# Gate and up weights of an expert in two runs of a slot in place of interleaved columns

## The reference

```python
def hier_moe(h, w_grp, b_grp, w_rtr, b_rtr, w_gate, w_up, w_down):
    ...                                   # gates: (tokens, 16), two of them not zero
    a = jnp.einsum('td,edf->tef', t, w_gate)      # w_gate, w_up: (16, 1024, 256) for a layer
    u = jnp.einsum('td,edf->tef', t, w_up)
    hid = jax.nn.silu(a) * u * gates.astype(t.dtype)[..., None]
    y = jnp.einsum('tef,efd->td', hid, w_down)    # w_down: (16, 256, 1024)
```

## Time and profile before

| | |
|---|---|
| median of 3 runs | 1561.44 us (1558.87 to 1562.86) |
| profiled execution: time, span | 1561.03 us, 1559.2 us |
| mean granted TensorE clock | 0.914 of full speed |
| busy: DVE, ACT, POOL | 46%, 26%, 15% of the span |
| q1 (SP's loads): packets, bytes | 111264, 175.39 MB |
| q0 (POOL's DMAs): packets, bytes | 21344, 70.08 MB |

### The profile page before, as it was taken

The page is one execution under the profiler, slowest core; times in us unless marked ns, Lnnn a source line. Parts: engine busy times, 40 slices in busy tenths (PEclk is TensorE's granted clock), DMA queues, the critical chain, the costliest instruction groups (busy, mean ns, idle before and its releaser), DMA issues.

```text
span 1559.2 us, 23096 instructions
## 1 busy us (share of the span) xinstructions
PE 1292.1 (83%) x8094; PEld 773.3 (50%) x8094; DVE 709.6 (46%) x1687; ACT 410.1 (26%) x929; POOL 229.4 (15%) x358
## 2 busy tenths in 40 slices
PE   4899978999998589888478998799999945986950
PEld 3455455777676444333244454577766733532420
DVE  0345425777544524232346443377664444422326
ACT  2110145666401111010121112466761100100112
POOL 3310111000111012210211100200002001110023
PEclk8899989999999689999879999899999966998985
DMA  9500577000314844999470014910004073299943
GB/s 334 205 13 1 184 267 199 1 2 28 122 41 156 312 157 118 359 378 381 174 271 12 1 37 157 321 29 1 20 10 149 28 270 107 83 362 381 367 165 146
DMA packets 132760, 247.54 MB, mean 159 GB/s; under 512 B 6688, under 2 KB 80672, under 8 KB 128512
## 3 DMA queue, kind: packets, MB, share of 16 engines
q1 hardware_dynamic: 111264, 175.39, 33.0%
q0 software_dynamic: 21344, 70.08, 12.6%
HBM read 217.17 MB, written 28.38 MB: 157 GB/s over the span
## 4 chain that ended last, share of the span: by engine, by line
PE 43%; DVE 9%; DMA 5%; issue 4%; SPq 3%; DVEq 1%; ACT 1%; POOL 0%; POOLq 0%; ACTq 0%
PE ps L2049 8%; PE ps L1767 8%; PE ps L1663 5%; PE ps L1946 4%; PE ps L2094 4%; PE ps L1826 3%; PE ps L2043 3%; PE ps L1879 3%; DMA ring<-in_moe_w_up 2%; SPq L516 2%; PE ps L2087 2%; PE ps L1683 1%; DVE ring L1290 1%; DMA h_rows<-work 1%; DMA hT_region<-h_rows,idx 1%
## 5 line engine op out<-in xcount | busy, mean ns | idle before, releaser
L1767 PE MATMUL ps<-ring,hT_region 128*128 128x512 f32 (+1 forms) x640 | 270.0, 578 | 1.7 <-ACT hT_region L917 1.7
L1290 DVE TENSOR_SCALAR_CACHE_REDUCE ring<-ps 128x768 f32<-128x768 f32 (+1 forms) x168 | 132.7, 820 | 148.8 <-PE ps L1826 119.1
L1767 PEld LDWEIGHTS ps<-ring,hT_region 128*128 128x128 f32 x640 | 121.1, 192 | 133.1 <-issue 132.3
L976 ACT ACTIVATE ring<-ring,negm 128x768 f32<-128x768 f32 (+1 forms) x168 | 137.7, 821 | 35.3 <-DVE ring L1290 35.2
L2049 PE MATMUL ps<-ring,hT_region 128*128 x304 | 140.7, 617 | 7.4 <-DVE hT_region L1605 4.8
L1946 PE MATMUL ps<-ring,hT_region 128*128 128x384 f32 (+1 forms) x480 | 141.8, 453 | 0.0
L1826 PE MATMUL ps<-arena,qT 64*128 64x384 f32 (+1 forms) x640 | 125.4, 510 | 4.7 <-DVE ring L1290 2.9
L1628 DVE COPY work<-ps 128x256 f32<-128x256 f32 x29 | 12.3, 424 | 223.4 <-PE ps L1663 223.4
L1946 PEld LDWEIGHTS ps<-ring,hT_region 128*128 128x128 f32 x480 | 89.8, 190 | 44.2 <-issue 0.7
L1879 PE MATMUL ps<-work,arena 128*64 128x128 f32 x1600 | 105.6, 278 | 6.0 <-ACT work L992 4.3
L2043 PE MATMUL ps<-ring,hT_region 128*64 x160 | 83.3, 681 | 32.0 <-issue 32.0
(11 more groups left out here) (304 smaller groups left out, 1711.8 us busy)
## 6 DMA issues: line engine op xcount, KB each, us to landing
ring<-in_w_mod SPq DMA_DIRECT2D x24, 2048.0 KB, 10.8
ring<-in_moe_w_gate SPq DMA_DIRECT2D x32, 1024.0 KB, 11.4
ring<-in_moe_w_up SPq DMA_DIRECT2D x32, 1024.0 KB, 13.5
arena<-in_moe_w_down SPq DMA_DIRECT2D x32, 1024.0 KB, 10.1
y_rows<-arena POOLq DMA_DIRECT2D x29, 512.0 KB, 6.5
ring<-in_w_in SPq DMA_DIRECT2D x6, 2048.0 KB, 18.8
arena<-mod_rows POOLq DMA_DIRECT2D x12, 512.0 KB, 6.9
h_rows<-work POOLq DMA_DIRECT2D x10, 512.0 KB, 3.0
```

What stands on the lines that cost most here:

```text
L976: act.activation(v, v, ACT.Exp, bias=negm[:, 2 * (k % 3) + m:2 * (k % 3) + m + 1], scale=-1.0, accum_out=sums[:, c:c + 1]).then_inc(exp_do ...
L1290: ts(o_, i_, -pair_of(p)[4], None, ALU.mult, ALU.min, accum_out=col).then_inc(m_ready, 1)
L1767: last = mm(ps[:, b, 0:n], hT[:, c, t * P:(t + 1) * P], w[:, c, :], start=(c == 0), stop=(c == KC - 1))
```

## The change

Gate and up each get one run of 2048 columns in the slot, where before their 256-column pieces took turns. The DMA of one matrix now writes, in each partition, 8 KB in one piece, as it also reads them; before it wrote eight pieces of 1 KB with a gap of 1 KB after each. The moving operand of a matmul in `gate_up`, before 512 columns in a row, is now two pieces of 256 columns that lie 2048 columns apart. The output's place is the same; its view only gets the same two dimensions.

```diff
             def gate_up_weights(l, e, to, landed):
-                dst = to.rearrange("p (c k n) -> p c k n", c=KC, k=2)
+                dst = to.rearrange("p (k c n) -> p k c n", k=2, c=KC)
                 for k, name in enumerate(("moe_w_gate", "moe_w_up")):
-                    sp.dma_start(dst[:, :, k, :], a[name].rearrange("l e (p c) f -> (l e) p c f", c=KC)[e]
+                    sp.dma_start(dst[:, k], a[name].rearrange("l e (p c) f -> (l e) p c f", c=KC)[e]
                                  ).then_inc(landed, 16)
...
-                        wa = ring[:, bass.ds(pe.snap(a_at[i] * 4096), 4096)].rearrange("p (c n) -> p c n", c=KC)
-                        g = ps[:, 2 + i % 2, :]
+                        wa = ring[:, bass.ds(pe.snap(a_at[i] * 4096), 4096)].rearrange("p (k c n) -> p c k n", k=2, c=KC)
+                        g = ps[:, 2 + i % 2, :].rearrange("p (k n) -> p k n", k=2)
                         h = hgT[i % 2]
 
                         def of_two(b):
-                            wb = slot[b].rearrange("p (c n) -> p c n", c=KC)
+                            wb = slot[b].rearrange("p (k c n) -> p c k n", k=2, c=KC)
                             for c in range(KC):
-                                mm(g[0:HALF, :], h[:, c, 0:HALF], wa[:, c, :], start=(c == 0), stop=(c == KC - 1))
-                                last = mm(g[HALF:P, :], h[:, c, HALF:P], wb[:, c, :],
+                                mm(g[0:HALF], h[:, c, 0:HALF], wa[:, c, :], start=(c == 0), stop=(c == KC - 1))
+                                last = mm(g[HALF:P], h[:, c, HALF:P], wb[:, c, :],
                                           start=(c == 0), stop=(c == KC - 1))
                             last.then_inc(gu_done[l], 1)
```

## The result

The changed kernel takes 1540.59 us (median of 4 runs, 1539.46 to 1541.46), the kernel before 1560.32 (4 runs): the ratio is 0.9878, 95% interval 0.9864 to 0.9893, 19.7 us less. The profiled execution took 1540.87 us, its span is 1539.1. The forecast was 1543 with a range of 1535 to 1554.

What follows compares the result with a forecast made beforehand. Expert stages were taken as bound first by TensorE, then by full DMA engines. Stalls shrink by 10.3 + 8.0 = 18.3 us, other terms 0: 1561.0 - 18.3 = 1542.7, said as 1543; range 1535 to 1554.

Steps and rivals of the forecast that it cites:

- The rate: Expert stages: gate and up loads go from 349 to 419 GB/s, 1.0 us less for each expert.
- Rival 2: Expert stages: half the gain is kept, by loads at about 385 GB/s or slots as bound; 1551 to 1553 us, chance 0.18.
- What reaches the end: Expert stages: shorter loads cut TensorE's stalls, 10.3 us in layer 0 after 0.7 off, 8.0 in layer 1.
- rival 4: TensorE after stalls: shrinking stalls no longer lower its clock, 1.7 us for each of some 5; 1533 us, chance 0.07.
- The fixed loads: Loads of experts 0 to 3, before the first tile: end 4 us earlier, taken at 0, between 2 gained and 1 lost.
- POOL's queue: Gathers and stores beside weight loads: longer packets shift engine time to SP's queue, hidden; taken at 0, bounds -2 and +3.
- rival 5: Gathers in expert stages come late, up to 3 us a tile for 14 tiles; 1585 us, chance 0.02.
- TensorE's reads: Passes in gate_up: the jump within 512 columns costs nothing; taken at 0, 25 us kept for the range.
- rival 1: TensorE pays for the jump in 288 passes of tiles without a stall: 1558 us at 53 ns each, chance 0.07.
- rival 3: Gate and up loads: packets stay at 1 KB, the row of 256 columns kept as a piece; 1561 us, chance 0.06.
- The page's rule of the Trainium skill: Gate and up loads: fixed 3 cycles a packet, so 7.5% shorter, 0.45 us an expert, 8 to 9 us in all.
- SP's issue: Issue of gate and up pairs gets shorter, but SP is waited for only while engines are full: 0, or a us at tile 7.

Runs made afterwards that it cites:

- Experiment 1: Changed kernel with each gate or up matrix in two DMAs, packets of 1, 2 or 4 KB: 1561.25, 1552.22 and 1543.5 us.
- second profile: The changed kernel measured once more, without further edits, beside the kernel before on another chip: 1539.56 us, ratio 0.9864.
- experiment 5: Kernel before, with the moving operand and output of gate_up walked in four pieces of 128 columns: 1559.81 us, ratio 1.0005.
- experiment 3: Register loads of a step's two experts put ahead of SP's slot wait: 1537.31 us in the changed kernel, 1556.51 in the kernel before.
- experiment 2: Changed kernel with four more SP register loads ahead of each expert: 1552.26 us; only from the second step with loads on: 1548.12.

## Why the prediction was right, step by step

**The rate.** Taken at 419 GB/s from the earlier trace rows, measured at 424. The row of the down loads was the right one to read. Experiment 1 shows that the rate goes with the packet length: it is back at 349 with 1 KB packets in the new layout.

Rival 2 falls with it and with the next step: neither the rate nor the slots took half of the gain.

**What reaches the end.** Forecast 10.3 us in layer 0 and 8.0 in layer 1; the distances shrank by 10.4 and 7.7. By tiles, layer 0, counted from tile 0: tile 7 2.0 forecast and 2.6 measured (88.9 to 86.4 us), tile 11 8.0 and 7.4 (148.9 to 141.5). Layer 1: tile 6 2.0 and 2.5 (74.3 to 71.8), tile 8 6.0 and 6.2 (108.9 to 102.7). In between it fits less well: tiles 8, 9 and 10 of layer 0 were to gain 2.5, 2.5 and 4.6 us and gained 3.8, 4.3 and 6.5. And the accounting in idle time was wrong. I said that the idle time would fall by 10 and 8 us, and it fell by 7.4 and 6.5; the stall of tile 11 was to be used up and rose from 3.44 to 4.22 us.

That forecast and measurement agree to 0.2 us is partly luck. By the measured rates 19 experts could save 1.06 us each, 20.2 in all, and 18.1 arrived: 2.1 us were lost where I had taken off 0.7, and the rate of 424 in place of 419 made up most of that. The changed kernel's second profile has 9.0 us in layer 0 in place of 10.4.

**The clock.** The rest came back as passes at the higher clock, what rival 4 describes. Five tiles got shorter by it: tiles 7, 10 and 13 of layer 0 by 1.0, 1.7 and 1.6 us, tiles 6 and 9 of layer 1 by 2.1 and 0.9, 7.3 us together. But, as I read it, a tile ahead of a later stall only ends sooner and then waits longer for its weights, so what it gained is inside the two distances; only tiles 13 and 9, behind which nothing stalls, add to them. Rival 4 counted some five such tiles at 1.7 us in full, and its 1533 did not come. Tile 10 took 8.82 us after 2.10 us of idle time before and no longer waits, which is 1.7 us. Tile 13 follows 2.02 us of idle time in place of 5.04 and its first pass takes 0.64 us in place of 1.11, with a granted clock of 1.00 of full speed (2.4 GHz) in its first 2 us, where before it was 0.50 (1.2 GHz): from tile 13 to tile 14 it is 13.6 us before and 12.0 after, 1.6 us that my sum did not have. The granted clock of the stretch rose from 0.94 to 0.97 of full speed. In layer 1 it is less, since tiles 8 and 9 still come after 5.04 and 3.31 us of idle time and still start at 1.11 us a pass: tile 9 takes 8.74 us in place of 9.61.

**The sum by place.** 1.0 us was there when tile 0 of layer 0 began, and already when SP issued the first of the changed loads (515.85 and 514.72 us), so not from the change. Then 10.4 (layer 0), 1.6 (tile 13's clock), 0.9 lost between the layers, 7.7 (layer 1), 0.9 (tile 9's clock) and 0.5 lost after it: 20.2 us, and the spans differ by 20.1. So 18.3 was forecast for steps that gave 18.1, 2.5 more came from the clock, and what is left varies between executions.

**The fixed loads.** Taken at 0. The loads ended 7 us sooner (42.8 us from the first issue to the last landing before, 35.8 after, where I had forecast 4), but the first gather shared the engines with longer packets and took 8.6 us in place of 8.3. That the conflict itself could be had for about 4 us, by holding one expert back, I had not seen.

**POOL's queue.** The turns by packet held, gathers land 2.6 us later, and nothing waits for them: rival 5 falls. I had read the earlier trace rows too coarsely: in the first 1.5 of those 5 us POOL's queue moved next to nothing, so its 1.05 MB took about 3.5 us beside 1 KB packets and not 5. Where both queues ran, in 687 to 688 us of that trace, they took turns there too:

```profile
q0 software_dynamic: 80, 0.33, 79.8%
q1 hardware_dynamic: 80, 0.08, 22.7%
```

**TensorE's reads** cost 0: rival 1 falls with experiment 5. **Packets** have 8 KB: rival 3 falls. The page's rule of the Trainium skill ("DMA: Bandwidth & Descriptors", section "Why small descriptors are slow (HBM only)"), 3 cycles a packet and so by estimate 8 to 9 us in all, gave under half of what came; measured were 9.5 ns a packet.

**SP's issue.** This step was mis-sized, though the sum did not show it. I wrote that SP is waited for only while the engines are full, with perhaps a us at tile 7. For the kernel before that nearly holds: experiment 3 finds 2.4 and 1.3 us at the first pair and nothing clear behind it. For the changed kernel it doesn't: experiment 2 shows that it loses some 11 us to 2.4 us of SP's time an expert. The 0.7 us that I took off for a queue that runs dry is the same mechanism, seen too small. How much of the 19.7 us is SP's shorter issue stays open: about 2 us by the estimate above, and the 6.6 us that are left with SP slower than before are not.

## What to carry to other kernels

When a stage is bound by the DMA engines, look at the length of the pieces on the slot's side of each load: a layout that takes them in one piece raised the rate from 349 to 424 GB/s here, and TensorE read it in two pieces at no cost. Read the new rate off a load in the same trace that already has the form. Once such a stage is faster, ask again who refills the queue: here the issuing engine's register loads and a collision with the first gather were worth another 7 us together.

## What the runs showed of the hardware

- With gate and up loads alone the 16 engines moved 349, 389, 409 and 424 GB/s in packets of 1, 2, 4 and 8 KB; all four fit 37.5 ns a KB and about 9.5 ns a packet on each engine.
- Two queues took turns by packet, with packets of 1 KB beside 4 KB (80 to 80) and of 8 KB beside 4 KB (155 to 154), so making one queue's packets longer takes bandwidth from the other: the median gather landed after 10.4 us in place of 7.8.
- A matmul's moving operand in two or four pieces took as long as one in a row: 592 ns a pass and 7.03 us for 16 passes at full clock.
- SP's issue of a 1 MB load into a queue with room took 0.6 us as 1024 packets and 0.35 us as 128. Twice the DMAs with the same bytes cost nothing that could be told at 4 KB packets (1543.5 us forecast from the rate, 1543.5 measured).
